# The last RMS norm of a two-block program: gain in the transposes, root and reciprocal, more of the sum on TensorE, two engines scale

## The chip, the cores and the metric

One core of one Trainium2 chip. The program is a single launch; the metric is its device time in microseconds (us). TensorE (PE), VectorE (DVE), ScalarE (ACT), GpSimd (POOL) and SyncE (SP) run their own instruction queues and meet at semaphores. Lower is better.

## What is computed

Two transformer-like blocks of width 1024 over 1024 tokens, in fp32: a pool and HGRN2 mixer with an MLP, then neighbourhood attention with a convolution and a gated feed-forward part. What the change touches is the end: the second block's down product, its residual, and the last norm.

```
def _rmsnorm(x, g):
    xf = x.astype(jnp.float32)
    y = xf * lax.rsqrt(jnp.mean(xf * xf, axis=-1, keepdims=True) + EPS)
    return (y * g.astype(jnp.float32)).astype(x.dtype)
...
        x = x + (jax.nn.gelu(gate, approximate=False) * val) @ w_down[l]
    return _rmsnorm(x, norm_f_g)
```

## The kernel before

**Layout.** The residual `x_t` is kept transposed: feature on the partition, 8 tiles `d` of 128 features (KT = 8), 1024 tokens along the row, in two halves `t` of 512 (HALF). The output has the token on the partition, so at the end every 128x128 block of `x_t` is turned by TensorE, and written to `y_tok`, 8 tiles of 128 tokens by 1024 features.

**The last loop.** The down products are made of groups of six matmuls (two rows of the hidden layer, three products of high and low parts). The last chunk of them is written out by hand, because the norm is woven into it: group `i` of 16 is the feature tile `d = i % 8` of the token half `t = i // 8`. TensorE (L1443 to L1463) does for each `i` the six matmuls (L1454) into one of four PSUM banks, and then `turn_back(i - 2)`: four transposes (L888 within `turn`) of the tile that was finished two groups earlier. After `i = 10` it does `sum_tokens(0)`, after the last group `turn_back(14)`, `turn_back(15)` and `sum_tokens(1)`.

**The other engines in that loop.** VectorE adds the PSUM bank to `x_t` (L2929). ScalarE squares the new tile (`square_out`, L2084) and copies the turned tile from PSUM to `y_tok` (`take_back`, L2090). GpSimd adds the squares of the tiles 1 to 6 of a half to the one of tile 0 (L820). `sum_tokens(t)` sums over the 128 partitions by a product with a column of ones: for each block of 128 tokens one matmul on GpSimd's sum (L1437) and one on the square of tile 7 (L1438), which yields the sum of squares with the token on the partition.

**The factor.** ScalarE then takes the logarithm of the mean (L2096) and its exponential with the factor -0.5 (L2102); each of the two needs another function table, so each is preceded by a table load. VectorE multiplies a tile of `y_tok` by this factor and by the gain in one pass (`scale_out`, L2922), the gain having been loaded as a 128x1024 tile of equal rows (`out_gain`). Tiles 0 to 3 depend on the first half alone, tiles 4 to 7 on the second. SP issues one DMA of 512 KB for each tile as it becomes ready (L709).

**What sets the order.** Everything here is written by hand, in the order of each engine's queue; there is no scheduler. The waits between the engines are on counting semaphores: `down_done` (product ready), `down_added` (residual added), `y_turned` and `y_copied` (transposes), `sq_ready` and `sq_summed` (squares), `norm_summed`, `mean_log`, `out_inv_ready` (factor), `out_ready` (scaled).

Of the kernel before, what the change touches and what calls it, by code (L numbers as in the profile page):

```python
# [27 lines left out]
ALU = mybir.AluOpType  # L28
# [111 lines left out]
T_DOWN2 = T_FFN + 2 * FT2  # L140

# [30 lines left out]
def two_blocks(nc, dram, out):  # L172
    ctx = ExitStack()
    with ctx:
# [166 lines left out]
        out_gain = at("out_gain", [P, D], A_ARENA + 32 * KB)  # L341
# [187 lines left out]
        out_gain_loaded = sem("out_gain_loaded")  # L529
# [113 lines left out]
        def _(sp):  # L643
# [63 lines left out]
            for t in range(KT):  # L707
                sp.wait_ge(out_ready, t + 1)
                sp.dma_start(out[0, t * P:(t + 1) * P, :], y_tok[:, t, :]).then_inc(stored, 16)  # L709
# [4 lines left out]
        def _(pool):  # L714
# [98 lines left out]
            for t in range(2):  # L813
                for d in range(1, KT - 1):
                    half = slice(t * HALF, (t + 1) * HALF)
                    pool.wait_ge(sq_ready, (5 + t) * KT + d + 1)
                    if d >= 2:

                        pool.wait_ge(sq_summed, SUMS_OUT + (KT - 2) * t + d - 1)
# [15 lines left out]
        def _(pe):  # L835
# [585 lines left out]
            def turn_back(i):  # L1421
# [6 lines left out]
                turn(x_t, i % 3, [x_t[:, d, t * HALF + c * P:t * HALF + (c + 1) * P] for c in range(4)], y_turned)  # L1428

            def sum_tokens(t):  # L1430


                pe.wait_ge(sq_summed, SUMS_OUT + (KT - 2) * (t + 1))
                pe.wait_ge(sq_ready, (5 + t) * KT + KT)
                for c in range(4 * t, 4 * t + 4):
                    tokens = slice(c * P, (c + 1) * P)
                    pe.matmul(psum[:, 3, c:c + 1], out_sq_sum[:, tokens], ones[:, 0:1], start=True, stop=False)  # L1437
                    last = pe.matmul(psum[:, 3, c:c + 1], out_sq[:, (KT - 1) % SQ_SLOTS, tokens], ones[:, 0:1],  # L1438
                                     start=False, stop=True)
                last.then_inc(norm_summed, 1)  # L1440


            pe.wait_ge(act_split, 2 * (MLP_CHUNKS + FFN_CHUNKS) + 2)  # L1443
            for i in range(2 * KT):
# [14 lines left out]
                if i == KT + 2:  # L1459
                    sum_tokens(0)  # L1460
            turn_back(2 * KT - 2)
            turn_back(2 * KT - 1)
            sum_tokens(1)  # L1463
# [3 lines left out]
        def _(act):  # L1467
# [600 lines left out]
            with act.Fori(0, (FFN_CHUNKS - 5) // 2) as i:  # L2068
# [5 lines left out]
            act.wait_ge(tile_done, T_END - 2)  # L2074
            act.dma_start(out_gain[:, :], bass.AP(dram["norm_f_g_2"].tensor, 0, [[0, P], [1, D]]))\
               .then_inc(out_gain_loaded, 16)

            def square_out(d, t):

                part = slice(t * HALF, (t + 1) * HALF)  # L2080
                if d > SQ_SLOTS:

                    act.wait_ge(sq_summed, SUMS_OUT + (KT - 2) * t + d - SQ_SLOTS)
# [9 lines left out]
            def log_out(t):  # L2093
# [894 lines left out]
```

## Time and profile before

| | |
|---|---|
| median of 3 runs | 2533.76 us (2530.29 to 2533.99) |
| the profiled execution's own time | 2534.9 us |
| its span in the trace | 2533.1 us |
| PE busy | 2489.2 us, 98% |
| DVE busy | 1686.6 us, 67% |
| ACT busy | 807.5 us, 32% |
| POOL busy | 1132.3 us, 45% |
| mean granted TensorE clock | 0.993 |

The span runs from the first to the last instruction or transfer; 1.8 us of the profiled execution's time lie around it. TensorE is busy in nearly the whole span, so the shares of the other engines say little about what sets the time; only at the very end does TensorE run out of work.

### The profile page before, as it was taken

To read this page: it belongs to the slowest core of one execution; us is meant where nothing else is said; L and a number is where in the kernel's file an instruction comes from. 1 tells how busy PE (TensorE), PEld (TensorE's weight loads), DVE (VectorE), ACT (ScalarE), POOL (GpSimd) and SP (SyncE) were. 2 spreads that over 40 slices of the span, in tenths; PEclk is the share of its full clock that TensorE was granted. 3 is DMA by queue.
4 is the path that set the end of the run, shared out by engine and by line. 5 is a ranking of instruction groups with operands and counts; after the bars stand their busy time and mean duration, and the time that the engine had idled before them with its cause. 6 is when DMAs were issued, how large, how long until landed. Compare 5 with 4: busy or idle time off the path is not lost.

```text
span 2533.1 us, 38526 instructions
## 1 busy us (share of the span) xinstructions
PE 2489.2 (98%) x14121; PEld 2040.0 (81%) x14121; DVE 1686.6 (67%) x1822; ACT 807.5 (32%) x1137; POOL 1132.3 (45%) x665
## 2 busy tenths in 40 slices
PE   8999998999999999999999999999999999999998
PEld 7788886878888788887877778888878888888886
DVE  6755556753334566657777779444789999987665
ACT  5233344343333000004133330411355444431003
POOL 2322222367876233333322223332369999863333
PEclk9999998999999999999999999999999999999998
DMA  5111112234424322221311111113222222243222
GB/s 211 42 42 33 33 33 93 100 113 121 134 99 149 125 99 99 91 99 49 118 40 39 31 33 50 45 48 125 92 84 83 91 75 83 91 146 119 99 94 80
DMA packets 221470, 217.48 MB, mean 86 GB/s; under 512 B 16303, under 2 KB 185946, under 8 KB 220378
## 3 DMA queue, kind: packets, MB, share of 16 engines
q1 hardware_dynamic: 189604, 122.92, 16.0%
q10 hardware_dynamic: 31798, 93.64, 10.0%
q8 instruction: 44, 0.72, 0.1%
q14 instruction: 24, 0.20, 0.0%
HBM read 167.24 MB, written 51.06 MB: 86 GB/s over the span
## 4 chain that ended last, share of the span: by engine, by line
PE 86%; DVE 8%; ACT 3%; issue 1%; DMA 1%; ACTq 0%; DVEq 0%; SPq 0%
PE psum L849 28%; PE psum L1134 27%; PE psum L868 21%; PE psum L1350 3%; PE psum L888 1%; PE psum L976 1%; PE psum L1279 1%; DVE h_lo L2144 1%; DVE sq_sum L2412 1%; PE psum L1454 1%; PE psum L1260 1%; DVE sq_sum L2139 1%; DVE sq_sum L2546 0%; PE psum L1035 0%; DVE x_t L2420 0%
## 5 line engine op out<-in xcount | busy, mean ns | idle before, releaser
L753 POOL CAST w_hi<-w_raw 128x1024 fp32r<-128x1024 f32 x136 | 151.4, 1114 | 1191.8 <-issue 624.1
L2448 DVE TENSOR_TENSOR x_t<-x_t,psum 128x512 f32<-128x512 f32 x416 | 284.0, 685 | 205.5 <-PE psum L868 197.1
L755 POOL TENSOR_TENSOR w_lo<-w_raw,w_hi 128x1024 fp32r<-128x1024 f32 x136 | 346.5, 2548 | 10.9
L849 PE MATMUL psum<-h_hi,w_hi 128*128 128x512 f32 x1040 | 335.1, 403 | 7.6 <-DVE h_lo L2247 6.3
L849 PE MATMUL psum<-h_lo,w_hi 128*128 128x512 f32 x1040 | 322.4, 391 | 0.0
L849 PE MATMUL psum<-h_hi,w_lo 128*128 128x512 f32 x1040 | 321.5, 390 | 0.0
L849 PEld LDWEIGHTS psum<-h_hi,w_hi 128*128 128x128 f32 x1040 | 189.8, 189 | 53.9 <-issue 16.4
L849 PEld LDWEIGHTS psum<-h_lo,w_hi 128*128 128x128 f32 x1040 | 196.0, 188 | 42.1
L849 PEld LDWEIGHTS psum<-h_hi,w_lo 128*128 128x128 f32 x1040 | 195.8, 188 | 42.2
L868 PE MATMUL psum<-down_hi,w_hi 128*128 128x512 f32 x512 | 199.6, 390 | 2.7 <-DVE x_t L2448 2.5
L868 PE MATMUL psum<-down_lo,w_hi 128*128 128x512 f32 x512 | 199.2, 389 | 0.0
L868 PE MATMUL psum<-down_hi,w_lo 128*128 128x512 f32 x512 | 199.2, 389 | 0.0
L2613 DVE SCALAR_TENSOR_TENSOR conv_t<-u_t,cols,conv_t 128x1024 f32<-128x1024 f32 x120 | 179.6, 1496 | 2.4
L804 POOL TENSOR_TENSOR ffn_s_lo<-ffn_s_sum,ffn_s_hi 128x512 fp32r<-128x512 f32 x84 | 159.3, 1926 | 8.6 <-ACT ffn_s_hi L1667 6.1
L868 PE MATMUL psum<-ffn_hi,w_hi 128*128 128x512 f32 x320 | 124.7, 390 | 0.5 <-DVE x_t L2448 0.5
L868 PE MATMUL psum<-ffn_lo,w_hi 128*128 128x512 f32 x320 | 124.5, 389 | 0.0
L868 PE MATMUL psum<-ffn_hi,w_lo 128*128 128x512 f32 x320 | 124.5, 389 | 0.0
L1781 ACT ACTIVATE down_hi<-down_in 128x1024 fp32r<-128x1024 f32 x32 | 32.1, 1052 | 281.1 <-DMA down_in<-act_rows 281.1
L868 PEld LDWEIGHTS psum<-down_hi,w_hi 128*128 128x128 f32 x512 | 96.1, 188 | 24.4 <-DVE x_t L2448 4.4
L868 PEld LDWEIGHTS psum<-down_lo,w_hi 128*128 128x128 f32 x512 | 96.1, 188 | 19.8
L868 PEld LDWEIGHTS psum<-down_hi,w_lo 128*128 128x128 f32 x512 | 96.1, 188 | 19.8
L1134 PE MATMUL psum<-ffn_t_hi,ffn_s_hi 128*128 128x512 f32 x252 | 98.1, 389 | 0.0
(448 smaller groups left out, 5561.4 us busy)
## 6 DMA issues: line engine op xcount, KB each, us to landing
w_raw<-in_w_in SPq DMA_DIRECT2D x124, 256.0 KB, 3.1
w_raw<-in_w_down SPq DMA_DIRECT2D x108, 256.0 KB, 2.7
w_raw<-in_w_up SPq DMA_DIRECT2D x76, 256.0 KB, 3.8
act_rows<-mlp_a ACTq DMA_DIRECT2D x32, 512.0 KB, 3.8
down_in<-act_rows ACTq DMA_DIRECT2D x32, 512.0 KB, 3.6
ffn_raw<-in_w_up SPq DMA_DIRECT2D x44, 256.0 KB, 3.7
ffn_rows<-ffn_gate ACTq DMA_DIRECT2D x22, 512.0 KB, 2.6
ffn_in<-ffn_rows ACTq DMA_DIRECT2D x22, 512.0 KB, 3.6
```

The lines of the kernel that those rows point to most:

```text
L753: pool.tensor_copy(hi, w_raw[:, slot, :]).then_inc(weight_hi, 1)
L755: pool.tensor_tensor(lo, w_raw[:, slot, :], hi.bitcast(F32), ALU.subtract).then_inc(weight_split, 1)
L804: done = pool.tensor_tensor(lo[:, :], full[c], hi[:, :].bitcast(F32), ALU.subtract)
L849: last = pe.matmul(psum[:, first_bank + t, :], w, a[:, k, t * HALF:(t + 1) * HALF], start=(k == 0 and j == 0), stop=(k == KT - 1 and j == 2))
L868: last = pe.matmul(psum[:, 4 + g % 4, :], w, a[k][:, t * HALF:(t + 1) * HALF], start=(k == 0 and j == 0), stop=(k == 1 and j == 2))
L888: last = pe.transpose(psum[:, dst_bank + c // 4, (c % 4) * P:(c % 4 + 1) * P], block_in, ident[:, :])
L976: last = pe.matmul(dst, e_t[:, l % 2, at_k:at_k + width], level_parts(e, l)[:, :, 1, :], start=True, stop=True)
L1134: last = pe.matmul(psum[:, bank, :], w, a[:, :], start=start and kk == part[0] and j == 0, stop=stop and kk == part[-1] and j == 2, skip_g ...
L1350: last = pe.matmul(psum[:, bank + t, :], w, a[:, t * HALF:(t + 1) * HALF], start=(k == 0 and j == 0), stop=(k == 3 and j == 2))
L1781: act.activation(down_hi[b][j][:, :], down_in[b][j][:, :], ACT.Copy).then_inc(act_hi_ready, 1)
L2448: dve.tensor_tensor(x_d, x_d, psum[:, 4 + g % 4, :], ALU.add).then_inc(down_added, 1)
L2613: dve.scalar_tensor_tensor(acc, u_t[:, c % 2, tap:tap + SEQ], w, acc, ALU.mult, ALU.add)\
```

## The change

**Gain.** The gain no longer multiplies a tile of the output. VectorE makes eight diagonal matrices `out_diag[:, d, :]` (the identity times the gain of feature tile `d`, a `tensor_scalar` each), after the add of group 11 of the chunk before the last. `turn_back` now does an ordinary fp32 matmul of the `x_t` block with that diagonal, which turns the block and multiplies it by the gain; before it was a transpose (`pe.transpose`) with the identity. The load of `out_gain` is gone.

**Sum of squares.** For the second token half GpSimd adds the squares 1 to 4 only; the squares 5, 6 and 7 are each summed by TensorE, four matmuls with the column of ones per square, between the last transposes. For the first half nothing changes but the order of the eight matmuls.

**Factor.** ScalarE takes the square root of the mean, VectorE its reciprocal. Logarithm and exponential are gone.

**Scaling.** A tile is multiplied by its factor alone (`tensor_scalar` instead of `scalar_tensor_tensor`). ScalarE scales the tiles 5 and 7 and issues their DMAs itself; VectorE scales the rest. The first tile is scaled after the add of group 12 instead of 13.

```diff
+DVE_TILES, ACT_TILES = (0, 1, 2, 3, 4, 6), (5, 7)
+OUT_SUMS = (KT - 2, KT - 4)
...
-        out_gain = at("out_gain", [P, D], A_ARENA + 32 * KB)
+        out_diag = at("out_diag", [P, KT, P], A_ARENA + 32 * KB)
...
-            for t in range(KT):
-                sp.wait_ge(out_ready, t + 1)
+            for i, t in enumerate(DVE_TILES):
+                sp.wait_ge(out_ready, i + 1)
                 sp.dma_start(out[0, t * P:(t + 1) * P, :], y_tok[:, t, :]).then_inc(stored, 16)
...
-                for d in range(1, KT - 1):
+                for d in range(1, OUT_SUMS[t] + 1):
                     half = slice(t * HALF, (t + 1) * HALF)
                     pool.wait_ge(sq_ready, (5 + t) * KT + d + 1)
                     if d >= 2:
-                        pool.wait_ge(sq_summed, SUMS_OUT + (KT - 2) * t + d - 1)
+                        pool.wait_ge(sq_summed, SUMS_OUT + OUT_SUMS[0] * t + d - 1)
                     pool.tensor_tensor(out_sq_sum[:, half], out_sq_sum[:, half], out_sq[:, d % SQ_SLOTS, half], ALU.add)\
                         .then_inc(sq_summed, 1)
...
-                turn(x_t, i % 3, [x_t[:, d, t * HALF + c * P:t * HALF + (c + 1) * P] for c in range(4)], y_turned)
-
-            def sum_tokens(t):
-
-
-                pe.wait_ge(sq_summed, SUMS_OUT + (KT - 2) * (t + 1))
-                pe.wait_ge(sq_ready, (5 + t) * KT + KT)
+                for c in range(4):
+                    tokens = slice(t * HALF + c * P, t * HALF + (c + 1) * P)
+                    last = pe.matmul(psum[:, i % 3, c * P:(c + 1) * P], x_t[:, d, tokens], out_diag[:, d, :],
+                                     start=True, stop=True)
+                last.then_inc(y_turned, 1)
+
+            def sum_tokens(t, src, start=False, stop=False):
+
                 for c in range(4 * t, 4 * t + 4):
-                    tokens = slice(c * P, (c + 1) * P)
-                    pe.matmul(psum[:, 3, c:c + 1], out_sq_sum[:, tokens], ones[:, 0:1], start=True, stop=False)
-                    last = pe.matmul(psum[:, 3, c:c + 1], out_sq[:, (KT - 1) % SQ_SLOTS, tokens], ones[:, 0:1],
-                                     start=False, stop=True)
-                last.then_inc(norm_summed, 1)
+                    last = pe.matmul(psum[:, 3, c:c + 1], src[:, c * P:(c + 1) * P], ones[:, 0:1],
+                                     start=start and c == 4 * t, stop=stop, skip_group_check=True)
+                if stop:
+                    last.then_inc(norm_summed, 1)
+
+            def sum_added(t):
+                pe.wait_ge(sq_summed, SUMS_OUT + sum(OUT_SUMS[:t + 1]))
+                sum_tokens(t, out_sq_sum, start=True)
+
+            def sum_square(t, d):
+                pe.wait_ge(sq_ready, (5 + t) * KT + d + 1)
+                sum_tokens(t, out_sq[:, d % SQ_SLOTS, :], stop=d == KT - 1)
             pe.wait_ge(act_split, 2 * (MLP_CHUNKS + FFN_CHUNKS) + 2)
+            pe.wait_ge(out_diag_ready, KT)
             for i in range(2 * KT):
                 d, t = i % KT, i // KT
                 if i >= 2:
                     turn_back(i - 2)
                 if i == KT + 2:
-                    sum_tokens(0)
+                    sum_added(0)
+                    sum_square(0, KT - 1)
+            sum_added(1)
+            sum_square(1, KT - 3)
             turn_back(2 * KT - 2)
+            sum_square(1, KT - 2)
             turn_back(2 * KT - 1)
-            sum_tokens(1)
+            sum_square(1, KT - 1)
...
-            act.wait_ge(tile_done, T_END - 2)
-            act.dma_start(out_gain[:, :], bass.AP(dram["norm_f_g_2"].tensor, 0, [[0, P], [1, D]]))\
-               .then_inc(out_gain_loaded, 16)
...
-            def log_out(t):
+            def root_out(t):
                 part = slice(4 * t, 4 * t + 4)
                 act.wait_ge(norm_summed, 6 + t)
-                act.activation(out_inv[:, part], psum[:, 3, part], ACT.Ln, scale=1.0 / D, bias=eps2[:, :])\
+                act.activation(out_inv[:, part], psum[:, 3, part], ACT.Sqrt, scale=1.0 / D, bias=eps2[:, :])\
                    .then_inc(mean_log, 1)
-
-            def inverse_out(t):
-                part = slice(4 * t, 4 * t + 4)
-                act.wait_ge(mean_log, 6 + t)
-                act.activation(out_inv[:, part], out_inv[:, part], ACT.Exp, scale=-0.5).then_inc(out_inv_ready, 1)
...
-                    log_out(0)
-                if i == KT + 4:
-                    inverse_out(0)
+                    root_out(0)
             take_back(2 * KT - 2)
             take_back(2 * KT - 1)
-            log_out(1)
-            inverse_out(1)
+            root_out(1)
+            act.wait_ge(out_inv_ready, 2)
+            act.wait_ge(y_copied, 2 * KT)
+            for i, t in enumerate(ACT_TILES):
+                act.activation(y_tok[:, t, :], y_tok[:, t, :], ACT.Copy, scale=out_inv[:, t:t + 1]).then_inc(y_copied, 1)
+                act.wait_ge(y_copied, 2 * KT + i + 1)
+                act.dma_start(out[0, t * P:(t + 1) * P, :], y_tok[:, t, :]).then_inc(stored, 16)
...
-            ffn_down_low(FFN_CHUNKS - 2, T_DOWN2 + 2 * (FFN_CHUNKS - 2), 1)
-
+
+            def out_diagonals():
+                for d in range(KT):
+                    dve.tensor_scalar(out_diag[:, d, :], ident[:, :], col("norm_f_g_2", d), None, ALU.mult)\
+                        .then_inc(out_diag_ready, 1)
+
+            ffn_down_low(FFN_CHUNKS - 2, T_DOWN2 + 2 * (FFN_CHUNKS - 2), 1, {11: out_diagonals})
+
+
+            def inverse_out(t):
+                part = slice(4 * t, 4 * t + 4)
+                dve.wait_ge(mean_log, 6 + t)
+                dve.reciprocal(out_inv[:, part], out_inv[:, part]).then_inc(out_inv_ready, 1)
             def scale_out(t):
                 dve.wait_ge(y_copied, KT * (t // 4 + 1))
                 dve.wait_ge(out_inv_ready, t // 4 + 1)
-                dve.scalar_tensor_tensor(y_tok[:, t, :], y_tok[:, t, :], out_inv[:, t:t + 1], out_gain[:, :],
-                                         ALU.mult, ALU.mult).then_inc(out_ready, 1)
+                dve.tensor_scalar(y_tok[:, t, :], y_tok[:, t, :], out_inv[:, t:t + 1], None, ALU.mult).then_inc(out_ready, 1)
             for i in range(2 * KT):
                 d, t = i % KT, i // KT
                 dve.wait_ge(down_done, 14 * (MLP_CHUNKS + FFN_CHUNKS - 1) + i + 1)
                 x_d = x_t[:, d, t * HALF:(t + 1) * HALF]
                 dve.tensor_tensor(x_d, x_d, psum[:, 4 + i % 4, :], ALU.add).then_inc(down_added, 1)
-                if i == KT + 5:
-                    dve.wait_ge(out_gain_loaded, 16)
-                if i >= KT + 5:
-                    scale_out(i - KT - 5)
-            for t in range(3, KT):
+                if i == KT + 4:
+                    inverse_out(0)
+                if KT + 4 <= i < 2 * KT - 1:
+                    scale_out(i - KT - 4)
+            scale_out(3)
+            inverse_out(1)
+            for t in DVE_TILES[4:]:
                 scale_out(t)
```

TensorE's queue after the last product, before: `ffn_hi` and `w_lo_last` belong to that product, `x_t` with `ident` is a transpose, `ones` marks the sums.

```order
L1454 MATMUL psum<-ffn_hi_1_496,w_lo_last 128x512
L888 MATMUL psum<-ident,x_t 128x128 [waits y_copied,down_added]
L888 MATMUL psum<-ident,x_t 128x128 x3
...
L1437 MATMUL psum<-ones,out_sq_sum 128x1 [waits sq_ready,sq_summed]
L1438 MATMUL psum<-ones,out_sq 128x1
```

The rows left out are two more groups of four transposes. And now:

```order
L1465 MATMUL psum<-ffn_hi_1_496,w_lo_last 128x512
L1432 MATMUL psum<-out_diag,x_t 128x128 [waits y_copied,down_added]
L1432 MATMUL psum<-out_diag,x_t 128x128 x3
L1439 MATMUL psum<-ones,out_sq_sum 128x1 [waits sq_summed]
L1439 MATMUL psum<-ones,out_sq_sum 128x1 x3
L1439 MATMUL psum<-ones,out_sq 128x1 [waits sq_ready]
L1439 MATMUL psum<-ones,out_sq 128x1 x3
...
```

In the place left out stand `turn_back(14)`, four matmuls on a square, `turn_back(15)` and four more. So three groups of turning products remain behind the last product, and the 8 matmuls with `ones` that stood at the very end have become 16, 12 of them ahead of the last four.

ScalarE's queue from the last squares on, before:

```order
L2084 ACTIVATE out_sq<-x_t 128x512 [waits sq_summed,down_added]
L2090 ACTIVATE y_tok<-psum 128x4x128 [waits y_turned] x3
L2096 ACT_TABLE_LOAD
L2096 ACTIVATE out_inv<-psum,eps_60 128x4 [waits norm_summed]
L2102 ACT_TABLE_LOAD
L2102 ACTIVATE out_inv<-out_inv 128x4 [waits mean_log]
```

and now:

```order
L2095 ACTIVATE out_sq<-x_t 128x512 [waits sq_summed,down_added]
L2101 ACTIVATE y_tok<-psum 128x4x128 [waits y_turned] x3
L2107 ACTIVATE out_inv<-psum,eps_60 128x4 [waits norm_summed]
L2124 ACTIVATE y_tok<-y_tok,out_inv 128x1024 [waits y_copied,out_inv_ready]
L2126 DMA out<-y_tok 128x1024 [waits y_copied]
L2124 ACTIVATE y_tok<-y_tok,out_inv 128x1024
```

No table load is left in this stretch (one stands earlier, ahead of the first half's root), and two tiles' scaling with their DMAs stands behind the root.

## Rows read from the trace of the kernel before

**Rows 1.** Chain that ended last, near the end: start us, us, what.

```profile
2486.03 4.08 PE psum L1454 x18
...
2499.26 0.44 PE psum L888 x4
2499.70 1.40 PE psum L1454 x6
```

**Rows 2.** Timeline of PE: start us, us, engine, line, operation, xcount.

```profile
2505.03 0.28 PE L1437 MATMUL psum<-ones,out_sq_sum 128*128 128x1 f32 x2
...
2506.74 0.48 PE L1454 MATMUL psum<-ffn_hi,w_hi 128*128 128x512 f32 x1
...
2514.05 0.48 PE L1454 MATMUL psum<-ffn_hi,w_hi_last 128*128 128x512 f32 x1
...
2515.53 0.60 PE L888 MATMUL psum<-ident,x_t 128*128 128x128 f32 x4
...
2518.64 0.71 PE L888 MATMUL psum<-ident,x_t 128*128 128x128 f32 x4 [1.57 <-DVE x_t L2929]
2519.39 0.56 PE L1437 MATMUL psum<-ones,out_sq_sum 128*128 128x1 f32 x2
```

**Rows 3.** Windows: us, busy by engine, then granted clock, DMA share, GB/s.

```profile
2517.00:2518.00 1.00, 0.07 (x1) 0.00 (x0) 1.00 (x2) 0.51 (x2) 0.90 (x1) 1.00 0.90 365
...
2519.00:2520.00 1.00, 0.96 (x6) 0.70 (x5) 1.00 (x1) 1.00 (x3) 0.11 (x1) 0.55 1.02 418
2520.00:2521.00 1.00, 1.00 (x6) 1.00 (x6) 1.00 (x2) 0.98 (x3) 0.00 (x0) 0.50 0.12 45
```

**Rows 4.** Timeline of ACT at the end of the program.

```profile
2522.97 0.26 ACT L2096 ACTIVATE out_inv<-psum,eps 128x4 f32<-128x4 f32 x1 [0.97 <-PE psum L1438]
2523.26 1.28 ACT L2102 ACT_TABLE_LOAD   x1
2524.55 0.20 ACT L2102 ACTIVATE out_inv<-out_inv 128x4 f32<-128x4 f32 x1
```

**Rows 5.** Timeline of DVE at the end of the program.

```profile
2517.91 0.67 DVE L2929 TENSOR_TENSOR x_t<-x_t,psum 128x512 f32<-128x512 f32 x1
...
2524.86 4.87 DVE L2922 SCALAR_TENSOR_TENSOR y_tok<-y_tok,out_inv,out_gain 128x1024 f32<-128x1024 f32 x4 [3.47 <-ACT out_inv L2102]
```

**Rows 6.** Windows of the last stores, and their issues (KB, us to landing).

```profile
2527.00:2528.00 1.00, 0.00 (x0) 0.00 (x0) 1.00 (x2) 0.00 (x0) 0.00 (x0) 0.50 1.04 422
...
2531.00:2532.00 1.00, 0.00 (x0) 0.00 (x0) 0.00 (x0) 0.00 (x0) 0.00 (x0) 0.50 1.01 414
...
out<-y_tok SPq DMA_DIRECT2D x8, 512.0 KB, 2.7
```

**Rows 7.** Timeline of PE in the first mixer, ordinary fp32 matmuls of 128x128.

```profile
134.37 0.39 PE L1037 MATMUL psum<-qd_t,states 128*128 128x128 f32 x2
...
136.38 0.39 PE L1035 MATMUL psum<-s_t,v_tok 128*128 128x128 f32 x2
```

**Rows 8.** Single lines: count of records, duration in ns min/median/max.

```profile
L1438 PE MATMUL psum<-ones,out_sq x16: 250/301/352, 2505.2 to 2522.6; 128*128 128x1 f32 x16
L888 PE MATMUL psum<-ident,x_t x64: 270/272/330, 2489.9 to 2519.0; 128*128 128x128 f32 x64
```

**Rows 9.** Single lines again: operations like the new ones on DVE and ACT.

```profile
L2551 DVE TENSOR_SCALAR sq_sum_gain<-sq_sum,gain_sq x1: 746/746/746, 1155.6 to 1155.6; 128x1024 f32<-128x1024 f32 x1
L2678 DVE RECIPROCAL row_inv<-row_sum x4: 243/247/248, 1290.7 to 1489.3; 128x16 f32<-128x16 f32 x4
L1860 ACT ACTIVATE qk<-qk,q_bias x4: 1154/1154/1155, 1244.4 to 1443.0; 128x1024 f32<-128x1024 f32 x4
L2600 DVE TENSOR_SCALAR near_mask<-near_mask x1: 360/360/360, 1225.5 to 1225.5; 128x384 f32<-128x384 f32 x1
```

**Rows 10.** Timeline of DVE in the chunk before the last.

```profile
2481.98 0.69 DVE L2448 TENSOR_TENSOR x_t<-x_t,psum 128x512 f32<-128x512 f32 x1 [0.67 <-PE psum L868]
```

More of the change, by code:

```diff
@@ L528, in two_blocks @@
         y_copied = sem("y_copied")
-        out_gain_loaded = sem("out_gain_loaded")
+        out_diag_ready = sem("out_diag_ready")
         out_inv_ready = sem("out_inv_ready")
@@ L2081, in square_out @@
                 if d > SQ_SLOTS:
-                    act.wait_ge(sq_summed, SUMS_OUT + (KT - 2) * t + d - SQ_SLOTS)
+                    act.wait_ge(sq_summed, SUMS_OUT + OUT_SUMS[0] * t + d - SQ_SLOTS)
                 act.activation(out_sq[:, d % SQ_SLOTS, part] if d else out_sq_sum[:, part], x_t[:, d, part], ACT.Square)\
```

## The prediction, made before the changed kernel was run

> **What bounds the kernel now.** The shares of the page say that TensorE is busy in 98% of the span, so I read the end of the program as a path: the chain of waits first, then the timelines of PE, ACT and DVE, the windows with the clock and, for the stores, the windows and the landing times.
>
> Three stretches come out. (a) Up to the end of the last product TensorE has no gap: the chain is the six matmuls of a group, 1.40 us, and four transposes, 0.44 us, in turn [rows 1]. Whatever is added to a group there is paid in full. The last product begins at 2514.05 and the transposes behind it at 2515.53, 1.48 us later [rows 2]. (b) Then TensorE waits: VectorE adds the last tile only at 2517.91, because it scales two tiles in between [rows 5]; the last transposes start at 2518.64 after a gap of 1.57 us, and the sums at 2519.39 [rows 2]. After this gap the granted clock goes from 1.00 through 0.55 to 0.50, that is from 2.4 to 1.2 GHz [rows 3], and the sums take until 2522.97, 3.58 us for 16 records (8 matmuls) [rows 2, 4]. The same 16 records at full clock took 2506.74 - 2505.03 = 1.71 us for the first half [rows 2]. (c) ScalarE needs 1.78 us from 2522.97 to 2524.75 for logarithm, table load and exponential [rows 4]; VectorE begins to scale at 2524.86 and takes 4.87 us for four tiles, 1.22 each [rows 5]. The first is ready at 2526.08, and the span ends 7.0 us later. In these 7 us the DMA engines are full: five windows in a row have a share of about 1 and 401 to 422 GB/s, the first and the last are shown [rows 6]. Four tiles of 512 KB at 410 GB/s are 5.1 us. So the end hangs on when the first tile of the second half is ready, hardly on how fast the others follow.
>
> **The change part by part.**
>
> *Turning by a product.* An ordinary fp32 matmul is recorded twice where a transpose is recorded once: the 8 matmuls of L1438 give 16 records, the 64 transposes of the tail 64 [rows 8]. Its price is in the first mixer: nine matmuls of 128x128 follow each other from 134.37 to 136.38, 0.223 us each [rows 7]; a transpose takes 0.44 / 4 = 0.11 [rows 1]. Four cost 0.89 instead of 0.44, so each group gets 0.45 us longer. Thirteen of the sixteen groups stand ahead of the last product: 13 x 0.45 = +5.85 us, all on TensorE without cover, and the last product begins at 2519.90 instead of 2514.05. The first turning group behind it starts at 2521.38.
>
> The Trainium skill's page "TensorE: Matmul & The Clock Gate", section "Terms", says that the transpose mode is four times faster for fp32. Rows 7 show a factor of two; by the page's factor each group would cost 1.32 us more instead of 0.45, and it is a rival below.
>
> *TensorE behind the last product.* Three turning groups, 3 x 0.89 = 2.67 us, and 16 matmuls with the column of ones, 32 records at 1.71 / 16 = 0.107 us, 3.42 us. What they wait for is there: the next to last add falls about 2519.3 and the last at about 2521.6 (VectorE has 1.4 us of work, an add and a scaling, in each group of 2.28 us, so it no longer runs late), GpSimd has four adds instead of six, and the squares come 0.7 us after the adds. TensorE therefore works through to 2521.38 + 6.09 = 2527.47, and ScalarE sees the sum 0.17 us later, as before (3.58 against 16 x 0.213): 2527.64. I take full clock here, since no gap lies ahead of these matmuls; that is the least certain value. At half clock the 6.1 us would be 12.2. Against before, 2522.97, this is +4.67 us: taking three squares off GpSimd saves nothing at the end, because TensorE now has more to do than the wait that goes.
>
> *The factor.* Root 0.26 us as the logarithm [rows 4], its table being loaded earlier; reciprocal of 128x4: bounds 0.20 (ScalarE's smallest operation [rows 4]) and 0.25 (a reciprocal of 128x16 [rows 9]), I take 0.25; 0.03 between them and 0.11 to the first scaling, as now between 2524.75 and 2524.86. In sum 0.65 instead of 1.89 us: -1.24.
>
> *Scaling.* VectorE multiplies 128x1024 by a column in 0.75 us [rows 9] instead of 1.22: the first tile is ready 0.47 earlier, at 2529.04. ScalarE's tile takes 1.15 [rows 9] and is ready at about 2529.4, VectorE's next at 2529.8, ScalarE's second at about 2531. All four come faster than the stores can carry them (1.28 us each), so the others gain nothing; the store queue of ScalarE only adds to the same full engines.
>
> *Work that is covered.* Eight diagonals on VectorE: a `tensor_scalar` of 128x384 takes 0.36 us [rows 9], and 128x128 less, so at most 8 x 0.36 = 2.9 us behind the add of group 11. Each group leaves VectorE 0.67 us [rows 10], and TensorE needs the delayed add only when it comes back to the same bank: the add of group 12 would be done by 2484.9 at worst, and the product that needs its bank begins at 2486.03 [rows 1]. So zero; without these spare banks it would be 2 us. The dropped load of `out_gain` and the earlier first scaling lie on no path: the first half's factor is due at about 2516.3, ahead of the add of group 13 at about 2517.0.
>
> *Sum.* +4.67 - 1.24 - 0.47 = +2.96 us. Span 2533.1 + 3.0 = 2536.1, profiled execution 2534.9 + 3.0 = 2537.9. The median of the runs is 1.1 below the profiled execution, so the forecast is 2533.76 + 2.96 = 2536.7 us. By this sum the program gets 0.12% slower, less than 0.2% (5.07 us), which is about what a measurement of this kernel can tell from no change.
>
> **The rivals.**
>
> *The clock falls behind the last product.* Slower. Before, 2.4 GHz held while TensorE had no gap, and fell after two gaps [rows 2, 3]. For the rival: half of the matmuls in these 6.1 us have a single moving column, and the longest such stretch at full clock in the trace is 1.71 us. Against it: no gap. Each microsecond's worth of work at half rate costs one more; from 2.1 us' worth on the loss exceeds 0.2%. If the second half of the stretch is slow, +3.05: +6.0, 2539.8 us; all of it, +9.1, 2542.8.
>
> The skill's same page, section "Part 4: PE-mode transpose", says that transposes do not count as TensorE work for the clock. By it the change from transposes to products helps to hold 2.4 GHz; no row here separates the two, since the loop held full clock with transposes in it.
>
> *Turning by a product costs no more than a transpose.* Then all sixteen differences of 0.45, 7.2 us, go: -4.2 us, 2529.5 us, 0.17% faster. Rows 7 and 8 speak against it.
>
> *It costs four times as much.* 16 x 1.32 = 21.1 us instead of 7.2: +16.9, 2550.7 us. Rows 7 speak against it.
>
> *The stores are not the limit.* Then the end is the last tile, ready at about 2531.0, plus 0.1 and the 2.7 us to landing [rows 6]: 2533.8 in the span, +0.7, 2534.5 us. The full DMA windows speak against it, since all stores share these engines.
>
> **How the numbers follow.** Forecast (+1.5 to +4.5 us) 0.65; clock 0.20, of which 0.05 stays under +5.07; cheap product 0.06; stores not the limit 0.07; fourfold price 0.02. Slower by over 0.2% is 0.15 of the clock, 0.02, and 0.03 of the forecast for terms that add up badly: 0.20. Faster by over 0.2% needs the cheap product and 1 us more: 0.03. The rest, 0.77, is within. For 8 in 10 the range leaves out the cheap product, the fourfold one and the worse half of the clock's cases; the low end reaches below the stores' case by the 3.7 us by which the runs before differ, in part: 2532 to 2541 us.
>
> **What would show it.** Turning groups of about 0.89 us and 8 records each, and the last product beginning 5.9 us later; TensorE without a gap from there to the last sum, with a granted clock of 1.00 in it; one table load in the tail instead of four; 0.65 us from the last sum to the first scaling; scalings of 0.75 and 1.15 us; then some 5 us of full DMA windows. I am wrong if the turning group stays at 0.44 us, if the clock falls before the last sum, or if the span ends much less than 7 us after the first scaled tile of the second half.

## The result, and the profile after

The changed kernel takes 2537.69 us, median of 21 runs (2533.34 to 2542.55), beside 2532.15 us, median of 21 runs of the kernel before (2528.95 to 2539.15). The ratio is 1.0022, with a 95% interval of 1.0016 to 1.0028: 5.5 us slower, where +2.96 was forecast. It lies at the very border between "no difference" and "slower by over 0.2%".

Single executions of one kernel differ by 9 to 10 us, most of it ahead of the output. So I compare, in the profiled executions, the **stretch from the first product of the last chunk to the end of the span**: 2485.9 to 2533.1 before, 47.2 us; 2481.8 to 2533.9 after, 52.1 us; +4.9 us. Its parts:

| part of the stretch | before | after | change | forecast |
|---|---|---|---|---|
| first to last product (starts) | 28.15 | 33.95 | +5.80 | +5.85 |
| start of the last product to the sum as ScalarE sees it | 8.92 | 9.85 | +0.93 | -1.18 |
| factor: sum to first scaling | 1.89 | 0.58 | -1.31 | -1.24 |
| first scaling | 1.22 | 0.71 | -0.51 | -0.47 |
| first scaled tile to the end | 7.0 | 7.0 | 0 | 0 |

One part is off, by 2.1 us: the second. (In the forecast +4.67 is the sum of the first two.)

The page of the changed kernel, the line of the span and that of the engines (busy us, share, instructions): its records on PE are more, its share of the span is still 98%.

```profile
span 2533.9 us, 38684 instructions
...
PE 2493.6 (98%) x14201; PEld 2046.0 (81%) x14201; DVE 1682.3 (66%) x1830; ACT 805.9 (32%) x1134; POOL 1128.7 (45%) x663
```

Timeline of PE after, at the end (start, us, line, operation, count). It answers [rows 2]. A turning group now has 8 records, 2514.94 to 2515.75, 0.81 us to the next product (0.89 where a sum follows). There is no idle time in brackets any more: the gap of 1.57 us is gone, as forecast. But the last three rows are stretched: the squares take 1.22 us (2520.79 to 2522.01) instead of 0.86, the last turning group 1.84 (2522.01 to 2523.85) instead of 0.89, the last squares 1.7 instead of 0.86 (the values behind "instead of" are those of the forecast). These are 2.1 us in sum.

```profile
2515.75 0.47 PE L1465 MATMUL psum<-ffn_hi,w_hi_last 128*128 128x512 f32 x1
...
2517.22 1.05 PE L1432 MATMUL psum<-out_diag,x_t 128*128 128x128 f32 x8
2518.11 0.95 PE L1439 MATMUL psum<-ones,out_sq_sum 128*128 128x1 f32 x8
2518.92 1.03 PE L1439 MATMUL psum<-ones,out_sq 128*128 128x1 f32 x8
2519.81 1.14 PE L1432 MATMUL psum<-out_diag,x_t 128*128 128x128 f32 x8
2520.79 1.36 PE L1439 MATMUL psum<-ones,out_sq 128*128 128x1 f32 x8
2522.01 2.05 PE L1432 MATMUL psum<-out_diag,x_t 128*128 128x128 f32 x8
2523.85 1.71 PE L1439 MATMUL psum<-ones,out_sq 128*128 128x1 f32 x8
```

Windows of the same place after (they answer [rows 3]) and of the stores ([rows 6]). A row has the busy time of PE, PEld, DVE, ACT and POOL, then the granted clock (1.00 is 2.4 GHz, 0.50 is 1.2), the DMA share and GB/s. In the first three rows PE and PEld are busy 1.00 throughout, and yet the granted clock, third number from the end, goes from 1.00 through 0.58 to 0.50. The stores are as before: windows with a DMA share of 1.00 and 0.99 at 401 and 393 GB/s.

```profile
2520.00:2521.00 1.00, 1.00 (x11) 1.00 (x10) 0.00 (x0) 0.01 (x1) 0.00 (x0) 1.00 0.90 365
2521.00:2522.00 1.00, 1.00 (x7) 1.00 (x7) 0.00 (x0) 0.58 (x1) 0.00 (x0) 0.58 0.07 16
2522.00:2523.00 1.00, 1.00 (x5) 1.00 (x6) 0.00 (x0) 0.00 (x0) 0.00 (x0) 0.50 0.00 0
...
2528.00:2529.00 1.00, 0.00 (x0) 0.00 (x0) 0.00 (x0) 0.83 (x1) 0.00 (x0) 0.50 1.00 401
...
2532.00:2533.00 1.00, 0.00 (x0) 0.00 (x0) 0.00 (x0) 0.00 (x0) 0.00 (x0) 0.50 0.99 393
```

Timelines of ACT and DVE after, in answer to [rows 4, 5]. The root (0.26) at 2525.60, the reciprocal (0.18) at 2525.89, the first scaling at 2526.18; no table load stands between them. VectorE's scalings take 0.71 us each (1.42 for two), ScalarE's 1.15.

```profile
2525.60 0.26 ACT L2107 ACTIVATE out_inv<-psum,eps 128x4 f32<-128x4 f32 x1 [0.90 <-PE psum L1439]
2526.11 1.15 ACT L2124 ACTIVATE y_tok<-y_tok,out_inv 128x1024 f32<-128x1024 f32 x1 [0.24 <-DVE out_inv L2937]
```

```profile
2525.89 0.18 DVE L2937 RECIPROCAL out_inv<-out_inv 128x4 f32<-128x4 f32 x1 [7.12 <-ACT out_inv L2107]
2526.18 1.42 DVE L2942 TENSOR_SCALAR y_tok<-y_tok,out_inv 128x1024 f32<-128x1024 f32 x2
```

The diagonals: the view of their line (ns min/median/max), and the operation of GpSimd that ran at their start.

```profile
L2928 DVE TENSOR_SCALAR out_diag<-ident,cols x8: 274/274/2129, 2477.2 to 2480.4; 128x128 f32<-128x128 f32 x8
```

```profile
2476.83 2.39 POOL L757 TENSOR_TENSOR w_lo_last<-w_raw,w_hi_last 128x1024 fp32r<-128x1024 f32 x1
```

Most took 0.274 us, one 2.129. From the start of the first to the end of the last there are 3.50 us (the records overlap), over my bound of 2.9. They cost nothing: TensorE has no gap between 2480 and 2484, and VectorE's adds are back in step by 2483.4.

### The profile page after: what moved, and what is told of

The parts are those of the page before. It is cut to its first block, busy times and chain, and to the rows that moved or that the text cites. A ratio compares the mean times of both kernels' runs of the same rounds, so it can differ in the third digit from the quotient of the medians.

```text
span 2533.9 us, 38684 instructions
## 1 busy us (share of the span) xinstructions
PE 2493.6 (98%) x14201; PEld 2046.0 (81%) x14201; DVE 1682.3 (66%) x1830; ACT 805.9 (32%) x1134; POOL 1128.7 (45%) x663
## 4 chain that ended last, share of the span: by engine, by line
PE 86%; DVE 8%; ACT 3%; DMA 2%; issue 1%; ACTq 0%; SPq 0%; DVEq 0%
PE psum L1136 27%; PE psum L851 27%; PE psum L870 21%; PE psum L1352 3%; PE psum L890 1%; PE psum L978 1%; PE psum L1281 1%; PE psum L1465 1%; DMA x_t<-x_spill 1%; DVE h_lo L2153 1%; DVE sq_sum L2421 1%; PE psum L1262 1%; PE psum L1432 1%; DVE sq_sum L2148 1%; DVE x_t L2429 0%
```

## The experiments

**The theories.** Mine, after the result: the sum of the prediction stands, each turning group costs 0.45 us more, and what failed is the clock behind the last product. Open is why it falls where TensorE has no gap. A first rival: the steps that shorten the end, root with reciprocal and scaling by two engines, bring less than the table says, and the turning costs less. A second: the end depends on GpSimd's adds, so that squares on TensorE save a wait. All lengths below are those of the stretch (before 47.2, after 52.1). Each of e1 to e8 is one profiled execution; e9 to e12 are timed besides.

### e1: the changed kernel with transposes, the gain left out

```diff
-                    last = pe.matmul(psum[:, i % 3, c * P:(c + 1) * P], x_t[:, d, tokens], out_diag[:, d, :],
-                                     start=True, stop=True)
+                    last = pe.transpose(psum[:, i % 3, c * P:(c + 1) * P], x_t[:, d, tokens], ident[:, :])
```

> The changed kernel, with the turning products made transposes with the identity again; the gain is left out of the computation. Read from the first product of the last chunk to the end of the span (47.1 us in the kernel before, 51.9 in the changed one). Theory (a turning product costs two transposes, and TensorE has no cover for it): a turning group takes 0.44 us instead of 0.89, the last product begins 5.8 us earlier, and the stretch is 43 to 44.5 us. Rival (the groups got longer through waits, on the diagonals or on y_tok): the turning groups stay near 0.9 us and the stretch above 50 us.

Measured: 43.7 us, 8.4 below the changed kernel. PE's timeline has turning groups of 4 records, 0.44 us (2513.08 to 2513.52):

```profile
2513.08 0.60 PE L1432 MATMUL psum<-ident,x_t 128*128 128x128 f32 x4
2513.52 0.95 PE L1438 MATMUL psum<-ones,out_sq_sum 128*128 128x1 f32 x8
...
2516.51 0.74 PE L1432 MATMUL psum<-ident,x_t 128*128 128x128 f32 x4
2517.04 1.71 PE L1438 MATMUL psum<-ones,out_sq 128*128 128x1 f32 x8
```

The clock falls here too, ahead of the last squares: 1.71 us for 8 records instead of 1.0, and 0.50 in the window.

```profile
2516.00:2517.00 1.00, 1.00 (x10) 1.00 (x10) 0.00 (x0) 0.49 (x1) 0.00 (x0) 0.95 0.90 365
2517.00:2518.00 1.00, 1.00 (x8) 1.00 (x6) 0.00 (x0) 0.60 (x1) 0.00 (x0) 0.50 0.00 0
```

So the turning is the price of the whole change: 16 groups at 0.45 us are 7.2 of the 8.4 us. Most of the other 1.2 us is clock: hardly more than the last squares ran at 1.2 GHz here. The fall of the clock is not the doing of the products with the diagonal.

### e2: the changed kernel, GpSimd adds six squares again, sums behind the last turning

```diff
-OUT_SUMS = (KT - 2, KT - 4)
+OUT_SUMS = (KT - 2, KT - 2)
...
-            sum_added(1)
-            sum_square(1, KT - 3)
             turn_back(2 * KT - 2)
-            sum_square(1, KT - 2)
             turn_back(2 * KT - 1)
+            sum_added(1)
             sum_square(1, KT - 1)
```

> The changed kernel, with GpSimd adding six squares for the second half again, and the sums (8 matmuls instead of 16) behind the last turning group. Theory (the squares summed on TensorE lengthen its queue by more than the wait for GpSimd did): the wait for GpSimd is under 0.5 us, the last sum is ready 3 to 4 us earlier after the last product, and the stretch from the first product to the end is 48 to 49 us instead of 51.9. Rival (TensorE would have waited for GpSimd's last add): a gap of over 2 us ahead of the sums, and a stretch of 51 us or more.

Measured: 48.2 us, 3.9 less than the changed kernel. PE's timeline: 24 turning records in a row, then 16 of the sums, with no idle time between, so no wait for GpSimd. The window of the last sums has the clock at 1.00.

```profile
2521.22 2.84 PE L1432 MATMUL psum<-out_diag,x_t 128*128 128x128 f32 x24
2523.90 0.95 PE L1439 MATMUL psum<-ones,out_sq_sum 128*128 128x1 f32 x8
2524.71 1.03 PE L1439 MATMUL psum<-ones,out_sq 128*128 128x1 f32 x8
```

```profile
2525.00:2526.00 1.00, 0.74 (x7) 0.66 (x6) 0.00 (x0) 0.22 (x1) 0.00 (x0) 1.00 0.07 16
```

From the last product to the sum as ScalarE sees it there are 6.0 us instead of 9.85. Two matmuls per token block fewer at full clock are 16 records, 16 x 0.107 = 1.7 us; the other 2.1 us are the clock. The second rival falls: the two squares put on TensorE save nothing in this kernel, they cost 1.7 us of work there, and without them the clock holds.

### e3: the sums with 128 columns of ones

```diff
-                    last = pe.matmul(psum[:, 3, c:c + 1], src[:, c * P:(c + 1) * P], ones[:, 0:1],
+                    last = pe.matmul(psum[:, 3, c % 4 * P:(c % 4 + 1) * P], src[:, c * P:(c + 1) * P], ones[:, :],
...
-                act.activation(out_inv[:, part], psum[:, 3, part], ACT.Sqrt, scale=1.0 / D, bias=eps2[:, :])\
+                act.activation(out_inv[:, part], psum[:, 3, 0:HALF:P], ACT.Sqrt, scale=1.0 / D, bias=eps2[:, :])\
```

> The changed kernel, with each sum over the partitions made with 128 columns of ones instead of one (the other 127 results are equal and not used). Theory A (the clock falls because products with one moving column leave TensorE nearly inactive although it is recorded busy): records stay near 0.11 us each, the granted clock stays at 1.00 to the last sum, and the stretch from the first product to the end is about 2.1 us shorter, 49.5 to 50 us. Theory B (the clock falls because the 128-column fp32 work as such counts too little): the clock falls at the same place, about 4 us after the last product, and the stretch stays at 51.9 us.

Measured: 50.1 us, 2.0 less. The sums are hardly longer for 128 columns than for one: 8 records in 0.89 us, against 0.81 and 0.89 in the changed kernel ahead of the fall. The last turning group takes 0.89 us (2523.20 to 2524.09) instead of 1.84:

```profile
2523.20 1.06 PE L1432 MATMUL psum<-out_diag,x_t 128*128 128x128 f32 x8
2524.09 1.06 PE L1439 MATMUL psum<-ones,out_sq 128*128 128x128 f32 x8
```

and the granted clock is 1.00 to the last of them:

```profile
2523.00:2524.00 1.00, 1.00 (x12) 1.00 (x11) 0.00 (x0) 0.10 (x1) 0.00 (x0) 1.00 0.00 0
2524.00:2525.00 1.00, 1.00 (x11) 0.96 (x9) 0.00 (x0) 0.60 (x1) 0.00 (x0) 1.00 0.00 0
```

PE is as busy as in the changed kernel, in the same order, with the same waits. What differs is the number of columns of the sums, and from the start of the last product to the sum there are 7.91 us instead of 9.85: 1.94 of the 2.1 us that the forecast had missed are back.

### e4: the kernel before with root and reciprocal alone

```diff
-                act.activation(out_inv[:, part], psum[:, 3, part], ACT.Ln, scale=1.0 / D, bias=eps2[:, :])\
+                act.activation(out_inv[:, part], psum[:, 3, part], ACT.Sqrt, scale=1.0 / D, bias=eps2[:, :])\
...
-                act.activation(out_inv[:, part], out_inv[:, part], ACT.Exp, scale=-0.5).then_inc(out_inv_ready, 1)
...
+                dve.wait_ge(mean_log, 6 + t)
+                dve.reciprocal(out_inv[:, part], out_inv[:, part]).then_inc(out_inv_ready, 1)
```

> The kernel before, with one part of the change alone: root on ScalarE and reciprocal on VectorE instead of logarithm and exponential. Theory: 0.58 us from the last sum to the first scaling instead of 1.89, nothing else moves on the path, and the stretch from the first product to the end is 45.6 to 46 us instead of 47.1. Rival (VectorE, which now waits for the root inside its queue, delays the adds): the last add comes later than 31.9 us after the first product, and the stretch is 47 us or more.

Measured: 43.4 us, 3.8 less than before and over 2 less than expected. From the sum to the first scaling there are 0.57 us, as in the changed kernel: the first rival falls for this step. The rest came from PE. With one table load fewer the first half's factor is there earlier: VectorE's first scaling starts 1.1 us ahead of the last product instead of 0.4 behind its start, and its last add 2.9 us behind that start instead of 3.9. The gap ahead of the last transposes is 1.13 us instead of 1.57, the smaller one of 0.29 is gone, and the sums take 1.96 us to ScalarE's root (2516.92 to 2518.88) instead of 3.58, at full clock:

```profile
2516.16 0.66 PE L888 MATMUL psum<-ident,x_t 128*128 128x128 f32 x4 [1.13 <-DVE x_t L2926]
2516.92 0.35 PE L1437 MATMUL psum<-ones,out_sq_sum 128*128 128x1 f32 x2
...
2518.48 0.36 PE L1438 MATMUL psum<-ones,out_sq 128*128 128x1 f32 x2
```

```profile
2517.00:2518.00 1.00, 1.00 (x10) 1.00 (x10) 1.00 (x2) 1.00 (x3) 0.00 (x0) 1.00 0.65 266
2518.00:2519.00 1.00, 0.84 (x8) 0.75 (x7) 0.92 (x1) 0.36 (x2) 0.00 (x0) 1.00 0.45 184
```

1.32 of the factor, 1.6 of the clock and 0.73 of the two gaps are 3.65 of the 3.8 us. My expectation counted the factor alone: a miss.

### e5: the changed kernel, VectorE scales all eight tiles

```diff
-DVE_TILES, ACT_TILES = (0, 1, 2, 3, 4, 6), (5, 7)
+DVE_TILES, ACT_TILES = (0, 1, 2, 3, 4, 5, 6, 7), ()
...
-            act.wait_ge(out_inv_ready, 2)
-            act.wait_ge(y_copied, 2 * KT)
```

> The changed kernel, with VectorE scaling all eight tiles. Theory (the last stores are bound by the DMA engines, so who scales the later tiles changes nothing): VectorE's four scalings follow in 0.7 to 0.8 us each, the stores fill the DMA engines as before, and the stretch from the first product of the last chunk to the end is 51.9 to 52.3 us, as in the changed kernel (52.1). Rival (two engines bring the end forward): 53 us or more.

Measured: 51.6 us, 0.3 under the expected range. One engine is no slower than two: VectorE scales the four tiles in 2.74 us, faster than the stores carry them, and from the start of the first scaling to the end there are 7.7 us, as with two. What is shorter lies ahead of it: the clock fell here too, with PE busy 1.00, but 5.9 us after the start of the last product instead of 5.4, and the sum came 9.41 us after that start instead of 9.85.

```profile
2529.44 2.74 DVE L2940 TENSOR_SCALAR y_tok<-y_tok,out_inv 128x1024 f32<-128x1024 f32 x4
```

### e6: the kernel before with its second scaling behind the last add

```diff
-                if i >= KT + 5:
-                    scale_out(i - KT - 5)
-            for t in range(3, KT):
+                if i == KT + 5:
+                    scale_out(0)
+            for t in range(1, KT):
```

> The kernel before, with one thing changed: VectorE scales the second tile of the first half behind the last add instead of ahead of it. Theory (the gap of TensorE that VectorE's late add makes is what lowers the clock): the last add comes about 1.7 us after the start of the last product instead of 3.9, no gap over 0.5 us lies ahead of the last transposes, the sums run at a granted clock of 1.00 in about 1.8 us instead of 3.6, though GpSimd's last add may now be waited for up to 1 us; the stretch from the first product to the end is 44.3 to 45.5 us instead of 47.2. Rival (the clock falls anyway about 4 us after the last product): it falls within the sums, and the stretch stays above 45.8 us.

Measured: 45.5 us, at the upper edge. I had expected no gap over 0.5 us ahead of the last transposes and found three smaller ones in place of the large one, each with another releaser: VectorE, ScalarE, GpSimd.

```profile
2511.01 0.66 PE L888 MATMUL psum<-ident,x_t 128*128 128x128 f32 x4 [0.29 <-DVE x_t L2929]
2512.25 0.63 PE L888 MATMUL psum<-ident,x_t 128*128 128x128 f32 x4 [0.58 <-ACT y_tok L2090]
2513.93 0.38 PE L1437 MATMUL psum<-ones,out_sq_sum 128*128 128x1 f32 x2 [1.05 <-POOL out_sq_sum L820]
```

```profile
2514.00:2515.00 1.00, 1.00 (x10) 1.00 (x10) 1.00 (x2) 0.98 (x2) 0.00 (x0) 1.00 0.89 360
```

Together they are 1.92 us, as long as the 1.86 of before (0.29 and 1.57), but none is as long as 1.57; the clock held through the sums, 1.98 us to ScalarE's logarithm instead of 3.58. These 1.6 us are nearly all of the 1.7 gained.

### e7: everything that helped, with transposes

Root and reciprocal as in e4, the second scaling behind the last add as in e6, the last two squares of the second half and the last of the first summed on TensorE, the sums with 128 columns; the transposes and the tile of the gain stay.

```diff
+OUT_SUMS = (KT - 2, KT - 3)
...
+            sum_added(1)
             turn_back(2 * KT - 2)
+            sum_square(1, KT - 2)
             turn_back(2 * KT - 1)
-            sum_tokens(1)
+            sum_square(1, KT - 1)
...
-                if i >= KT + 5:
-                    scale_out(i - KT - 5)
-            for t in range(3, KT):
+                if i == KT + 5:
+                    scale_out(0)
+            for t in range(1, 4):
+                scale_out(t)
+            inverse_out(1)
+            for t in range(4, KT):
                 scale_out(t)
```

> The kernel before with root and reciprocal (as the part alone, 43.4 us in the stretch), VectorE's second scaling behind the last add, squares 6 and 7 of the second half summed on TensorE, and all sums made with 128 columns of ones. Transposes and the gain tile stay. Theory: no gap of TensorE behind the last product, granted clock 1.00 to the last sum, the last sum seen about 5.6 us after the start of the last product, 0.58 us to the first scaling, and a stretch of 42.2 to 42.9 us. Rival (GpSimd or the squares are late, so a gap comes back): 43.2 us or more.

Measured: 42.8 us, 4.4 less than before and 9.3 less than the changed kernel. No gap on PE, clock 1.00 to the last sum, which ScalarE sees 5.8 us after the start of the last product:

```profile
2514.07 0.60 PE L889 MATMUL psum<-ident,x_t 128*128 128x128 f32 x4
2514.55 1.16 PE L1434 MATMUL psum<-ones,out_sq_sum 128*128 128x128 f32 x8
...
2517.31 1.06 PE L1434 MATMUL psum<-ones,out_sq 128*128 128x128 f32 x8
```

### e8: e7 with the first tile of the second half in two pieces

```diff
+OUT_PIECES = [(t, slice(0, D)) for t in range(4)] + [(4, slice(0, 512)), (4, slice(512, D))] + [(t, slice(0, D)) for t in range(5, KT)]
...
-            for t in range(4, KT):
-                scale_out(t)
+            for t, part in OUT_PIECES[4:]:
+                scale_out(t, part)
```

> As e7_transposes_kept, with the first tile of the second half scaled and stored in two halves of 512 columns. Theory (the end is the readiness of the first output behind the last sum, plus the full DMA engines): the stores start 0.5 to 0.6 us earlier and so does the end, 41.7 to 42.3 us. Rival (halves cost fixed times on VectorE and in the queue): no shorter than e7_transposes_kept.

Measured: 42.8 us, nothing gained where about 0.6 to 1 us was expected. DVE's timelines, of e7 and of e8:

```profile
2518.99 4.87 DVE L2927 SCALAR_TENSOR_TENSOR y_tok<-y_tok,out_inv,out_gain 128x1024 f32<-128x1024 f32 x4
```

```profile
2520.57 5.00 DVE L2928 SCALAR_TENSOR_TENSOR y_tok<-y_tok,out_inv,out_gain 128x512 f32<-128x512 f32 x5
```

The last tile is scaled at 2523.86 in e7 and 2525.57 in e8, and the ends of the spans, 2527.2 and 2528.8, lie 3.3 and 3.2 us behind. The first store may start earlier, but the DMA engines then run short; the window of e8 shows a share of 0.89 and 332 GB/s:

```profile
2523.00:2524.00 1.00, 0.00 (x0) 0.00 (x0) 1.00 (x2) 0.00 (x0) 0.00 (x0) 1.00 0.89 332
```

With the gain in the scaling, a tile each 1.22 us is hardly faster than the 1.28 us of its store, so the last tile binds about as much as the first. There is a second reason, which these two runs don't part from the first. Behind the last add stand the scalings of three tiles of the first half, too, and in e7 the nine windows from 2517 to 2526 have a DMA share of at least 0.90 each; with the last one they carry 3.67 MB, seven tiles without a pause. In e8 the windows are as full when the first piece is ready (2521 to 2522: 1.00), so its store found the engines busy. "Only the first tile counts" is true of tiles that come each 0.7 us to DMA engines that stand idle, as in the changed kernel.

### e9 to e12: the changed kernel, e3, e4 and e7, timed on one chip

e9 is the changed kernel again, e10 is e3, e11 is e4 and e12 is e7; the edits are those above.

> The changed kernel once more, timed beside the three below, and for a second trace. If the fall of the clock belongs to this kernel's last sums, the granted clock reaches 0.50 before the last sum again, about 4 us after the last product, and the stretch from the first product of the last chunk to the end is 51.5 to 52.3 us; if it was chance, the clock holds and the stretch is about 50 us. Time against before: 1.0015 to 1.0030.

> The changed kernel with sums of 128 columns of ones once more. Theory A (one moving column lets the clock fall): the clock holds to the last sum again, the stretch is 49.8 to 50.4 us, and the median lies about 2 us below that of the changed kernel in this job, ratio to before 1.0008 to 1.0016. Theory B (chance): no steady difference from the changed kernel.

> The kernel before with root and reciprocal alone, timed. By the stretch, 43.4 us instead of 47.2, it should be 3.8 us faster than before, ratio 0.9980 to 0.9990. If the clock's holding in it was chance, the ratio is 0.9990 to 0.9995.

> Root and reciprocal, second scaling behind the last add, squares 6 and 7 on TensorE, wide sums, transposes and gain tile kept; timed. By the stretch, 42.8 us instead of 47.2, 4.4 us faster than before, ratio 0.9976 to 0.9988, and 9 to 10 us faster than the changed kernel.

| kernel | median us (11 runs; before 33) | ratio to before, 95% | stretch us |
|---|---|---|---|
| before | 2533.34 | | |
| e9, changed | 2537.42 | 1.0020 (1.0011 to 1.0029) | 51.3 |
| e10, changed with wide sums | 2537.58 | 1.0019 (1.0010 to 1.0028) | 50.0 |
| e11, root and reciprocal alone | 2530.62 | 0.9987 (0.9978 to 0.9996) | 43.3 |
| e12, transposes kept | 2528.91 | 0.9985 (0.9976 to 0.9994) | 42.8 |

e11 and e12 are faster than both kernels, with ratios in the expected ranges. The interval of e11 holds the case of the factor alone (0.9990 to 0.9995) as well, so its time doesn't show the part of the clock. e12 is 8.5 us below e9, under the expected 9 to 10; the stretches give the same, 51.3 - 42.8 = 8.5. Between e11 and e12 the times don't decide.

e10 against e9 is a miss: 2 us were expected and the medians show none. The windows repeat the difference. In e9 the clock falls before the last sum, with PE at 1.00:

```profile
2523.00:2524.00 1.00, 1.00 (x12) 1.00 (x11) 0.00 (x0) 0.41 (x1) 0.00 (x0) 1.00 0.57 217
2524.00:2525.00 1.00, 1.00 (x9) 1.00 (x9) 0.00 (x0) 0.19 (x1) 0.00 (x0) 0.81 0.00 0
2525.00:2526.00 1.00, 1.00 (x8) 1.00 (x6) 0.00 (x0) 0.07 (x1) 0.00 (x0) 0.50 0.00 0
```

In e10 it holds to the last sum:

```profile
2528.00:2529.00 1.00, 1.00 (x11) 1.00 (x10) 0.00 (x0) 0.60 (x1) 0.00 (x0) 1.00 0.00 0
```

The stretches differ by 1.3 us here and by 2.0 in e3, while the 11 runs of each kernel lie 5 and 9 us apart. So the gain of the wide sums is shown in the traces (7.91 us from the start of the last product to the sum in e3 and in e10; 9.85, 9.41 and 9.08 in the changed kernel, e5 and e9) and not in the times.

## Why the prediction came out as it did

- **What bounds it, and the turning by a product.** Right. 13 groups ahead of the last product gave +5.80 us against +5.85, from a price read 2370 us earlier in the program [rows 7]. e1 takes this part back and the gain with it. The rivals of a cheap and of a fourfold price are out, and so is the figure of the Trainium skill's "TensorE: Matmul & The Clock Gate", section "Terms": the factor here is 0.89 / 0.44 = 2.
- **TensorE behind the last product.** This is the term that failed: I took full clock, named it the least certain value, and got 9.85 us instead of 7.74, 2.1 us more. In the other two traces with this order it is 1.7 (e5) and 1.3 (e9), since the clock fell 5.9 and 6.3 us after the start of the last product and not 5.4: the fall came every time, its moment moved. The work itself was counted rightly: e3 and e10, at full clock, need 0.89 us for each group of 8 records. The reason for full clock ("no gap lies ahead") was wrong: the clock fell in the changed kernel, e5, e9 and e1 without any gap. The rival's mechanism came about in part, later than in its milder case of +3.05 us. With it the sum is 2.96 + 2.1 = 5.1 us, beside +4.9 in the stretch, 5.5 in the medians and 4.1 in those of e9.
- **The rule on transposes** (the Trainium skill's "TensorE: Matmul & The Clock Gate", "Part 4: PE-mode transpose": a transpose does not count as busy for the clock in the way a matmul does). No run here shows it or contradicts it, and it did not decide anything: with transposes (e1) and with products (changed, e5, e9) the clock fell behind the last product; what held it was wider sums or fewer of them.
- **The factor.** -1.31 against -1.24. The reciprocal took 0.18 us, just under my lower bound of 0.20. e4 shows the step alone; there it brought far more, since the earlier factor of the first half also moved VectorE's scalings and its last add forward, and the clock held longer.
- **Scaling.** 0.71 us and 1.15 us as forecast; -0.51 against -0.47. The second engine brings nothing (e5), as the sum had it.
- **The stores.** Right: 7.0 us from the first scaled tile to the end, with full DMA windows. e8 shows where the rule ends.
- **The diagonals.** My bound, 8 x 0.36 = 2.9 us, was too low: one of them took 2129 ns, 3.50 from first start to last end. Covered all the same.
- **The chances.** No difference had 0.77 and slower by over 0.2% had 0.20; the ratio, 1.0022, is just beyond the bound, and its interval holds it. The range in us held the time, since it was cut for a part of the clock's cases. That the median lies only 1.0 above the forecast of 2536.7 is luck: the median of the kernel before came out 1.6 lower than the value I started from, so the change itself was missed by 2.6 us. A chance of 0.20 for the clock was too low for a value that I had called the least certain, with a row against it that I read as a matter of gaps alone [rows 3].

**What stays open.** In the kernel before the clock fell about 2519.1, ahead of its sums and behind gaps of 0.29 and 1.57 us; in e4 and e11 (1.13 and 1.14) and in e6 (0.29, 0.58 and 1.05) it held through the sums. It held only just: it fell 0.8 us behind the last sum in e4, 0.9 behind it in e6, and in e11 during the last record of the sums, which ends at 2521.50:

```profile
2521.00:2521.50 0.50, 0.50 (x5) 0.41 (x4) 0.50 (x1) 0.00 (x0) 0.00 (x0) 0.94 0.57 229
```

Counted from the start of the last product it fell after 5.1 us before, 7.1 in e4, 6.3 in e11 and 8.1 in e6. Two executions of one kernel (e4 and e11) are 0.9 us apart here, and the kernel before has only one kept trace, so part of the 1.6 us that the clock gave in e4 may be chance. That the length of the single gap decides would fit as well, but each is one execution or two, and no run changed the gap alone. Nor was it tried whether it is the single column of the sums as such or their number that counts: e2, with 16 one-column records at the end instead of 32, held too.

## What to carry to other kernels

On an engine that has no gap, a scaling hidden in a transpose is not free: a plain fp32 product costs two records where the transpose costs one, 0.45 us per group of four, sixteen times; what it saves, 0.5 us in the first scaling, it saves once. Try each part of a combined change by itself: here root with reciprocal alone wins 0.13%, and the whole loses 0.2%. At the end of a kernel a second engine or a smaller first tile gained nothing here, where the stores keep the DMA engines full (e5, e8).

## What the runs showed of the hardware that was not expected

- TensorE's granted clock can fall to 1.2 GHz while PE and PEld show 1.00 busy. It fell so behind the last product in the changed kernel, e5, e9 and e1, whose 32 records of sums behind that product have a single moving column, and held to the last sum in e3, e10, e7, e8 and e12, whose sums have 128, and in e2 with 16 of a single column.
- A record of an fp32 matmul with a 128x128 weight takes 0.10 to 0.11 us at 2.4 GHz with one moving column (8 in 0.81 to 0.89 us) and 0.11 with 128 (8 in 0.89): the narrow one is hardly cheaper.
- On VectorE one `tensor_scalar` of 128x128 took 2129 ns instead of 274; it started at 2477.17 while a subtraction of GpSimd ran (2476.83 to 2479.22), and ended 0.1 us after it. In e1, e2, e3, e5, e9 and e10, too, one of the eight takes 2128 to 2143 ns, and the first begins 0.3 us after the start of that subtraction. That the one waited for the other is only inferred from the times.
